# Cached-sequence attention in 16 half-sequence units, with the linear attention's pieces between their parts

## The reference, cut to what matters

```python
# gated linear attention, by chunk, all 512 prompt tokens and the new tokens
o = einsum("bihk,bhkv->bihv", qc * exp(b), s)
att = einsum("bihk,bjhk,bijhk->bijh", qc, kc, decay)
o = o + einsum("bijh,bjhv->bihv", att, vc)
s = s * exp(b_last)[..., None] + einsum("bjhk,bjhv->bhkv", kc * exp(b_last[:, None] - b), vc)
...
# attention of the new tokens over the cached rows (latent 128 wide, rotated key 32 wide)
kv_past = cache_kv_latent[i][page_table].reshape(bs, -1, MLA_KV_LORA)
kr_past = cache_k_rope[i][page_table].reshape(bs, -1, MLA_ROPE)
s = einsum("bqhr,bkr->bhqk", ql, kv) + einsum("bqhd,bkd->bhqk", qr, kr)
p = softmax(s * MLA_SCALE)                  # over 4096 cached and the new keys
o_lat = einsum("bhqk,bkr->bqhr", p, kv)
```

## Time and profile before

| | us |
|---|---|
| median of 3 runs (2382.7 to 2384.95) | 2383.07 |
| the profiled execution's own time | 2382.49 |
| its span in the profile | 2380.7 |
| TensorE matmuls busy, mean granted clock | 2054.9 (86%), 0.875 |
| VectorE, ScalarE, GpSimd busy | 946.1, 773.8, 654.3 |

### The profile page before, as it was taken

The page is one execution under the profiler, slowest core; times in us unless marked ns, Lnnn a source line. Parts: engine busy times, 40 slices in busy tenths (PEclk is TensorE's granted clock), DMA queues, the critical chain, the costliest instruction groups (busy, mean ns, idle before and its releaser), DMA issues. The chain is left out here.

```text
span 2380.7 us, 39144 instructions
## 1 busy us (share of the span) xinstructions
PE 2054.9 (86%) x16191; PEld 1864.0 (78%) x16191; DVE 946.1 (40%) x1477; ACT 773.8 (33%) x1395; POOL 654.3 (27%) x332
## 2 busy tenths in 40 slices
PE   4998887589779999989959987847979899999996
PEld 3997654468778999989859965536868799999995
DVE  2332433744332333345426044365433133333553
ACT  4333223243242322233344241323332422222433
POOL 0341100511222344434214310023103223443440
PEclk8998756589789999999979976656989999999998
DMA  2431001145012223222032210030722032322210
GB/s 88 136 63 38 7 5 59 44 175 195 29 56 75 86 71 106 70 92 98 10 104 89 28 44 0 6 102 6 281 87 71 28 106 72 101 75 97 76 63 38
DMA packets 168754, 177.23 MB, mean 74 GB/s; under 512 B 47198, under 2 KB 151302, under 8 KB 166340
## 3 DMA queue, kind: packets, MB, share of 16 engines
q1 hardware_dynamic: 163884, 132.58, 18.2%
q0 software_dynamic: 4608, 41.95, 4.8%
q10 hardware_dynamic: 100, 0.46, 0.1%
HBM read 166.11 MB, written 8.86 MB: 73 GB/s over the span
## 5 line engine op out<-in xcount | busy, mean ns | idle before, releaser
L337 POOL TENSOR_TENSOR w_low<-ring,w_high 128x1024 fp32r<-128x1024 f32 x120 | 290.7, 2424 | 613.8 <-ACT w_high L333 613.8
L356 PE MATMUL ps<-x_high,w_high 128*128 128x272 f32 x1664 | 346.7, 290 | 28.3 <-DVE x_low L347 22.3
L333 ACT ACTIVATE w_high<-ring 128x1024 fp32r<-128x1024 f32 x166 | 174.8, 1055 | 537.3 <-PE ps L356 483.1
L356 PE MATMUL ps<-x_low,w_high 128*128 128x272 f32 x1664 | 343.3, 287 | 0.0
L356 PE MATMUL ps<-x_high,w_low 128*128 128x272 f32 x1664 | 342.1, 287 | 0.0
L356 PEld LDWEIGHTS ps<-x_high,w_high 128*128 128x128 f32 x1664 | 260.8, 189 | 30.0 <-DVE x_low L347 23.2
L356 PEld LDWEIGHTS ps<-x_low,w_high 128*128 128x128 f32 x1664 | 262.6, 189 | 0.0
L356 PEld LDWEIGHTS ps<-x_high,w_low 128*128 128x128 f32 x1664 | 261.6, 188 | 0.0
L356 PE MATMUL ps<-x_high_in,w_high 128*128 128x272 f32 x736 | 154.1, 291 | 45.3 <-POOL w_low_in L337 45.3
L2532 DVE TENSOR_SCALAR arena<-arena,parb 128x560 f32<-128x560 f32 x44 | 84.4, 1919 | 271.4 <-ACT arena L2480 271.4
L337 POOL TENSOR_TENSOR w_low_in<-ring,w_high 128x1024 fp32r<-128x1024 f32 x46 | 109.8, 2389 | 271.5 <-ACT w_high L333 271.5
(11 more groups left out here) (398 smaller groups left out, 3517.4 us busy)
## 6 DMA issues: line engine op xcount, KB each, us to landing
ring<-in_ffn_w_up SPq DMA_DIRECT2D x44, 1024.0 KB, 5.5
ring<-in_ffn_w_down SPq DMA_DIRECT2D x20, 1024.0 KB, 5.1
ring<-in_w_in SPq DMA_DIRECT2D x18, 1024.0 KB, 5.3
ring<-in_w_out SPq DMA_DIRECT2D x8, 1024.0 KB, 8.1
ring<-in_ple_w_gate SPq DMA_DIRECT2D x8, 1024.0 KB, 5.2
big<-in_state_ssm SPq DMA_DIRECT2D x16, 256.0 KB, 4.2
out_ssm_sample<-big SPq DMA_DIRECT2D x4, 1024.0 KB
arena<-in_x_prompt SPq DMA_DIRECT2D x1, 2048.0 KB
```

The source lines that it names most:

```text
L333: act.activation(wh[:, i % 2], ring[:, n % RING, :, c0:c0 + P], ACT.Copy).then_inc(s_high, 1)
L337: pool.tensor_tensor(low[:, i % 2], ring[:, n % RING, :, c0:c0 + P], wh[:, i % 2].bitcast(F32), ALU.subtract).then_inc(s_low, 1)
L356: last = pe.matmul(ps[:, b + h, 0:HALF], w[:, i % 2, k, :], x[:, k, h * HALF:(h + 1) * HALF], start=(k == 0 and x is x_high and w is wh), ...
```

## The change

The cached block is merged into the linear block, with one order for each engine.

- The unit of the cached attention is half a sequence, `u` from 0 to 15: 16 rows a partition, gathers of 1 MB and 0.25 MB, three slots, all in the ring. The gather of unit `u + 2` is issued when the latents of `u - 1` are done, and behind GpSimd's piece of linear work for `u`.
- Transposes use three banks in turn instead of four. One bank each is left for scores, latents, linear tokens and outputs, linear attention, and state additions; none is doubled.
- All five transposed groups of a unit are copied by ScalarE; VectorE copies the one group of probabilities. `kvT` and `krs` are doubled by unit, `PTb` too. `own_max` and `exps` work on 512 columns.
- Between the parts of unit `u` stand the linear pieces: `tokens` and `updates` in even units, `attention` and `outputs` in odd ones, from 1 to 11; the norm in 12 and 13; the new keys' work in 13 to 15. The norm is made once for prompt and new tokens together.
- The state additions mask the keys by chunk (128 x 8 columns) instead of the values (256 x 8): 32 matmuls of 64 columns replace 4 of 512.
- The merge has nine parts instead of five, with 8 x 3 matmuls. The softmax statistics are kept for each half.
- All four `w_out` loads start when the last unit's latents are done, and two small copies of the new keys are added at the end of the stage before.

```diff
--- before.py
+++ after.py
...
+    put("eighth", 2 * (q % 4)[:, None] + np.arange(2)[None, :])
...
+                    def new_keys():
+                        act.activation(ckvT_new, ckvT[:, SEQ:T], ACT.Copy)
+                        act.activation(krT_new, krT[0:32, SEQ:T], ACT.Copy)
...
+            B_T, B_S, B_P, B_TO, B_AT, B_UP = (0, 1, 2), 3, 4, 5, 6, 7
...
+            groups = [g for u in range(NU + 1) for g in ([(u, c) for c in range(5)] if u < NU else [])
+                      + ([(u - 1, PROBS)] if u else [])]
...
+            def tbank(u, c):
+                return B_T[place[u, c] % 3]
...
-                    load_out(e, L, LD_OUT + RING - 1)
...
+                    e.wait_ge(s_pv2, NU)
+                    for n in range(LD_OUT, LD_OUT + RING):
+                        start_load(e, n % RING, [(ring[:, n % RING, :, :],
+                                                  w_cols(a["w_out"], L, 0, KD, 256 * (n - LD_OUT),
+                                                         256 * (n - LD_OUT + 1)))])
...
+                    def updates(j):
...
                         e.wait_ge(s_vk, 2 * j + 2)
-                        e.wait_ge(s_vm, j + 1)
-                        if j >= 2:
-                            e.wait_ge(s_st, 1 + 8 * (j - 1))
-                        for h in range(4):
-                            last = pe.matmul(ps[32 * h:32 * h + 32, b_upd[i2], :].rearrange("p (c v) -> p c v", c=8),
-                                             gkt[i2][0:n, 32 * h:32 * h + 32], gVm[i2][0:n, :, 64 * h:64 * h + 64],
-                                             start=True, stop=True)
+                        e.wait_ge(s_km, j + 1)
...
+                        if j:
+                            e.wait_ge(s_st, 1 + 8 * j)
+                        else:
+                            e.wait_ge(s_lu, 1)
+                        for c in range(8):
+                            for h in range(4):
+                                last = pe.matmul(ps[32 * h:32 * h + 32, B_UP, 64 * c:64 * c + 64],
+                                                 gKm[i2][0:n, c, 32 * h:32 * h + 32], gvt[i2][0:n, 64 * h:64 * h + 64],
+                                                 start=True, stop=True)
                         last.then_inc(s_gu, 1)
...
+                    def across(u, c):
+
+                        k = place[u, c]
+                        if k >= 3:
+                            e.wait_ge(*kept(*groups[k - 3]))
+                        if c == 0:
+                            e.wait_ge(s_kv[u % KV], L * KV_LAYER[u % KV] + 32 * (u // KV + 1))
+                        if c == PROBS:
+                            e.wait_ge(s_ex2, u + 1)
...
+                            last = pe.transpose(ps[:, tbank(u, c), q * P:(q + 1) * P], src, ident)
+                        last.then_inc(s_tr, 1)
...
+                    def scores(u):
+                        b = u // 2
+                        e.wait_ge(*kept(u, 4))
+                        if u:
+                            e.wait_ge(s_ex2, u)
...
+                    def latents(u):
+                        e.wait_ge(*kept(u, PROBS))
+                        if u:
+                            e.wait_ge(s_ol2, u)
+                        for q in range(4):
...
+                        last.then_inc(s_pv2, 1)
...
+                    def linear_first(u):
+                        j = u // 2 - 1
+                        if u in (2, 4, 6, 8):
+                            tokens(j + 1)
+                        if u in (3, 5, 7, 9, 11):
+                            attention(j)
+                        if u == 13:
+                            new_scores()
+                        if u == 14:
+                            new_probs()
+                        if u == 15:
+                            new_outputs()
+
+                    def linear_second(u):
+                        j = u // 2 - 1
+                        if u == 1:
+                            tokens(0)
+                        if u in (2, 4, 6, 8, 10):
+                            updates(j)
+                        if u in (3, 5, 7, 9, 11):
+                            outputs(j)
+                        if u == 12:
+                            sums_of_squares()
+
+                    gate()
+                    for c in range(5):
+                        across(0, c)
+                    scores(0)
+                    for u in range(1, NU):
+                        for c in range(5):
+                            across(u, c)
+                        linear_first(u)
+                        across(u - 1, PROBS)
+                        linear_second(u)
+                        scores(u)
+                        latents(u - 1)
+                    across(NU - 1, PROBS)
+                    latents(NU - 1)
...
+                    for b in range(NSEQ):
+                        pe.matmul(ps[:, 6, 16 * b:16 * b + 16], Ob[:, 0, b, :], Wsel[:, 0, b, :], start=(b == 0),
+                                  stop=False, skip_group_check=True)
+                        pe.matmul(ps[:, 6, 16 * b:16 * b + 16], Ob[:, 1, b, :], Wsel[:, 1, b, :], start=False,
+                                  stop=False, skip_group_check=True)
+                        last = pe.matmul(ps[:, 6, 16 * b:16 * b + 16], On[:, b, :], Wn[:, b, :], start=False, stop=True,
+                                         skip_group_check=True)
+                    last.then_inc(s_yy, 1)
...
+                    def keep(u, c):
+
+                        e.wait_ge(s_tr, place[u, c] + 1)
+                        if u >= 2:
+                            e.wait_ge(s_sc2, u - 1)
...
+                    def exps(u):
+                        e.wait_ge(s_mx2, u + 1)
+                        if u:
+                            e.wait_ge(s_tr, place[u - 1, PROBS] + 1)
+                        act.activation(Pb, ps[:, B_S, :], ACT.Exp, bias=nmx[:, u % 2, u // 2:u // 2 + 1],
+                                       scale=SCALE_MLA, accum_out=lsum[:, u % 2, u // 2:u // 2 + 1]).then_inc(s_ex2, 1)
+
+                    def kept_output(u):
+                        e.wait_ge(s_pv2, u + 1)
+                        act.activation(Ob[:, u % 2, u // 2, :], ps[:, B_P, 0:R], ACT.Copy).then_inc(s_ol2, 1)
...
+                    gates()
+                    for c in range(5):
+                        keep(0, c)
+                    decays(0)
+                    exps(0)
+                    for u in range(1, NU):
+                        for c in range(5):
+                            keep(u, c)
+                        linear(u)
+                        exps(u)
+                        kept_output(u - 1)
+                    kept_output(NU - 1)
...
+                    gates()
+                    differences(0)
+                    own_max(0)
+                    for u in range(1, NU):
+                        linear_first(u)
+                        keep_probs(u - 1)
+                        linear_second(u)
+                        own_max(u)
+                    keep_probs(NU - 1)
...
-                    def values_by_chunk(j):
+                    def keys_by_chunk(j):
                         n, i2 = gtiles[j][1], j % 2
-                        e.wait_ge(s_vk, 2 * j + 1)
+                        e.wait_ge(s_vk, 2 * j + 2)
...
-                        pool.tensor_tensor(gVm[i2][0:n], gvt[i2][0:n].unsqueeze(1).to_broadcast([n, 8, 256]),
...
+                        pool.tensor_tensor(gKm[i2][0:n], gkt[i2][0:n].unsqueeze(1).to_broadcast([n, 8, P]),
+                                           cm.unsqueeze(2).to_broadcast([n, 8, P]), ALU.mult).then_inc(s_km, 1)
+
+                    def linear(u):
+                        j = u // 2 - 1
+                        if u == 1:
+                            keys_by_chunk(0)
+                            times_keys(1)
+                        if u in (4, 6, 8):
+                            times_keys(j + 1)
+                        if u in (2, 4, 6, 8):
+                            keys_by_chunk(j + 1)
+
+                    for u in range(KV):
+                        gather(u)
                     times_keys(0)
-                    values_by_chunk(0)
-                    times_keys(1)
-                    for j in range(1, TT):
-                        values_by_chunk(j)
-                        if j + 1 < TT:
-                            times_keys(j + 1)
...
+                    for u in range(1, NU - KV + 1):
+                        linear(u)
+                        e.wait_ge(s_pv2, u)
+                        gather(u + KV - 1)
+                    for i in range(KV):
                         e.wait_ge(s_kv[i], L * KV_LAYER[i] + KV_LAYER[i])
...
```

766 lines of the change are left out of this document (342 added, 424 removed).

## The result

| | us |
|---|---|
| before, median of 4 runs beside the changed kernel's (2382.7 to 2385.86) | 2384.01 |
| after, median of 4 runs (2397.47 to 2408.28) | 2400.86 |
| ratio, 95% interval | 1.0070, 1.0047 to 1.0092 |
| the profiled execution of after: its time, its span | 2408.28, 2406.4 |

The account below looks back on a forecast made before the run. TensorE bounds the cached stage, a four-engine chain the linear stage; half units become loop-bound. Layer 0's block ends at 617.2 against 619.8: 2.6 less 1.1 behind it saves 1.5 us a layer, 3 in both: 2380 us, range 2356 to 2412.

Parts of the forecast that it names:

- a slot is back 7.85 us after its latents: Gather round trip in the merged block: 0.3 us to wake, issue over 1.24 us, 6.3 us to land.
- The even unit: Units 2, 4, 6, 8 with token transposes and state updates: 7.9 us, of it updates 1.75 and scores 1.75.
- the median of 6.3: Landing time of a 1 MB gather, on the straight line between 4.3 us (0.5 MB) and 10.2 us (2 MB).
- Units 4 to 9: Layer 0 sum: three pairs of an even unit (7.9 us) and an odd unit (15.0 us), 68.7 us.
- the 2 us for the clock: Added to each odd unit's 12.9 us because the granted clock falls in attention (ends 0 and 4.5), giving 15.0.
- Tail: Merge after the last latents: 14.5 us before, plus 4.3 for 8 matmul pairs and about 1.1 for statistics: 19.9.
- Behind the block: GpSimd clears 51 semaphores instead of 24, delaying w_low by 1.7 us, of which 1.1 us shows.
- B: Rival: clock stays low through odd units' outputs and scores, next unit starts cold; 22 us in all, 2402; chance 0.19.
- A: Rival: clock holds through odd units, 12.9 us each instead of 15.0; about 17 us less, 2363; chance 0.20.
- C: Rival: half gathers take as long as whole ones (10.2 us); about 25 us a layer, 2430; chance 0.08.
- the 8 us that I had named as a sign: Sign that the forecast is wrong: gathers of 1 MB landing later than 8 us.
- D: Rival: transposes at half rate throughout, 0.91 instead of 0.455 us a group; 2421; chance 0.03.

Follow-up runs that it names:

- issue_first: Changed kernel, VectorE's product with the queries of units 4, 6, 8 and 10 held until GpSimd has issued the previous unit's gathers: 2388.5 us, ratio 1.0016.
- rope_early: Changed kernel, a slot's rope rows gathered once its old ones are transposed, ahead of GpSimd's linear work; latents' rows still await the slot's latents: 2374.8 us, 0.9953.
- warm_waits: Changed kernel plus unread identity transposes on TensorE, 28 ahead of unit 5 and 20 each ahead of units 7 and 9: 2396.3 us, ratio 1.0053.
- fourth_slot: Changed kernel with a fourth gather slot laid over SSD outputs and state, so its output is wrong; same amount of work: 2363.1 us, ratio 0.9903.
- linear_apart: Changed kernel with all linear attention pieces ahead of the units on every engine, then 16 plain half units: 2452.1 us, ratio 1.0268.

## Why the prediction was wrong

**The step that failed** is "With 0.3 us to wake, a slot is back 7.85 us after its latents", and what was made of it. The prediction set this round trip only against two plain units, and put no wait into the odd units that carry `attention`. The even unit that has to cover it was priced at 7.9 us, so the margin was 0.05 us, and nothing was added for the case that it was missed. Measured in layer 0, issue to use was 11.75, 10.24 and 9.24 us for units 5, 7 and 9, thus 12.05, 10.54 and 9.54 with the 0.3 to wake, and the even unit that covers it was 7.2 us. The differences are the waits of 4.87, 3.36 and 2.36. Of these 10.6 us,

- 5.7 are the issue, held 1.9 us each time by VectorE's product (issue_first takes that away: 12.3 us in all);
- 2.9 are the use, 8.6, 7.1 and 6.1 us after the latents' issue where I had put the median of 6.3. Without rope rows just ahead of them the latents landed 5.5 to 5.9 us after issue from unit 5 on, the held 1.9 taken off (rope_early, 26 us in all). Why the landing of unit 5 was slower than that of unit 9, with rope rows ahead of both, isn't settled;
- 2.0 are the even unit, 0.7 us shorter each time than priced.

And each wait can be paid again by half-rate transposes, 2.04 us behind the first and 1.46 behind the second (warm_waits shows the mechanism). With a slot to spare all of the waits go (fourth_slot: 37.7 us). The earlier trace rows shows VectorE's operations slowed beside GpSimd's product, and I had priced that; that VectorE's product can hold GpSimd's issue I had not asked, and no issue in the kernel before shows it. Where two terms cancel to 0.05 us, the range of each is the forecast.

The sum by its own milestones, in us from the start of the block in layer 0 (ends of `scores`):

| | forecast | measured |
|---|---|---|
| unit 3 | 63.8 | 63.1 |
| unit 9 | 132.5 | 140.6 |
| unit 15 | 183.3 | 195.1 |
| end of the block | 207.5 | 218.9 |

*Start.* Unit 0 was to wait till 12.6 us after the block's start, and did (419.46 less 406.8). Unit 3 came 0.7 us early, although it waited 6.73 us for its rows, where the forecast left about 1 (457.9 less 456 and 0.9 for the latents): unit 2 ended its scores 41.1 us after the start, not 46.3. *Units 4 to 9* took 77.5 us instead of 68.7. Waits are 10.6 of them (4.87, 3.36, 2.36), slow transposes behind the waits 3.5 (4.50 and 3.92 us where 2.46 is usual); without both it is 63.4, so my unit prices were 5.3 too high. Even units took 7.2 instead of 7.9, as the updates took 0.92 us in line and not 1.75. Odd units, without the waits and the slow part of the transposes, took 14.0 on the mean against 15.0 (the terms that the prediction names for 12.9 add up to 12.5). With the transposes as they were, the odd units of layer 0 took 15.3, 15.8 and 14.4 us beside their waits, so the 2 us for the clock paid for this cost there; in layer 1 it didn't, with 15.9, 17.5 and 17.5. *Units 10 to 15* took 54.5 instead of 50.8, with 2.1 of waits; unit 13 took 12.5 instead of 10.2. *Tail.* 19.3 us against 19.9 forecast, right,'s pairs again near 0.5 us. *Behind the block* the first `w_low` starts 3.7 us after the block's end, 2.9 before (622.71 less 619.8): 0.8 later, forecast 1.7. TensorE's first product follows 6.4 us after the block's end, 6.0 before: 0.4 of it shows, forecast 1.1. The `w_out` loads landed 9.0 us after issue, not 8, and the tail hid them.

```profile
629.43 2.62 POOL L327 TENSOR_TENSOR w_low<-ring,w_high 128x1024 fp32r<-128x1024 f32 x1 [39.55 <-ACT w_high L323]
```

**The rivals.** B gave 2402, the nearest number, and a part of its mechanism shows. The first outputs (L1728) take 1.97 us in unit 5 above, as cold as in the earlier trace rows, and all outputs of units 7 and 9 take 3.6 us in line, the cold price. But `scores` behind them run warm or nearly so: two rows of 1.06 us in unit 5, at most 0.5 us more in the others, where unit 13's, in a colder stretch, took 1.93 each. In layer 0 no odd unit paid the 2.5 to 3 us of B. In layer 1 units 7 and 9 did (17.5 us), though by `attention` and the transposes and not by `scores`. That is 5 us in all, against 38 us of waits for rows behind unit 0, so the number of B was mostly luck. A had 12.9 us an odd unit. In rope_early, less their 1 us of wait, units 5 and 7 took 13.0 and 12.8 us and unit 9 14.6: A's price holds where the transposes start warm and the clock lasts. C is refuted: 6.3 us to land in the median, as forecast; one gather, unit 5's in layer 0, passed the 8 us that I had named as a sign. D is refuted: units 9 to 15, and the plain units of linear_apart, show 2.46 to 2.49 us for 20 transposes. So the odd units were late by a rival that I had not put down: a round trip with no margin, and no price for the case that its two numbers came out the wrong way round.

**The mask by chunk** I had only priced inside the merged block. It is worth 12 us on its own, so the kernel without merging and with this part was the better half of the change.

## What to carry to other kernels

A slot that comes back "just in time" needs its slack stated with its sign: add what can hold the issuing engine, what is queued ahead on the same queue, and the cold start behind the wait, and if the sum is not clearly below the cover, forecast a wait in every turn. Ask for the small piece of a slot as soon as that piece is free, so that the large piece is first in the queue when it is released; here that alone turned 0.7% slower into 0.5% faster. And when a change has several parts, price each alone: one of them may carry the whole gain.

## What the runs showed of the hardware that I had not expected

The issue of an indirect gather on GpSimd took 2.83 us beside a VectorE product of two on-chip operands (2.28 us), and 0.94 without it, whichever of the two gathers it was. The third gather of rope rows in each layer took 3.4 us (from 416.86 in layer 0) beside two VectorE operations from 416.56 to 420.15. TensorE's wait of 4.87 us was followed by 20 transposes in 4.50 us, half rate; transposes of a constant in the gap brought them to 2.43, at a granted clock of 1.00 instead of 0.50. VectorE's differences took 5.09 us beside GpSimd's mask of 3.61 us and 2.74 beside one of 1.91. 64 small matmul instructions of 64 columns (the updates) passed in 0.92 us (474.24 to 475.16), 14 ns each, against 1.75 us that 64 of 128 columns had suggested.
